# Gate and convolution projections as 2x2 blocks with seven products, kept in DRAM, ahead of the merges

## Chip, cores and metric

One core of a Trainium2 chip runs the whole kernel. The metric is the device time of one execution in microseconds (us). TensorE (PE) multiplies; VectorE (DVE), ScalarE (ACT) and GpSimd (POOL) work element by element; the queue of SyncE (SP) issues the transfers. 0.2% is 4.2 us.

## The reference

One layer on a sequence of 1024 rows of 1024 floats. Everything is float32.

```
h = rms_norm(x, norm1_g)
a_b, a_c, a_x, q, kv, nsa_g, pool_in, sgu_in, merge_g = split_columns(h @ w_in)
out_a = a_b * causal_dwconv(a_c * a_x, conv_a_w)          # 512 wide
out_b = nsa_mixer(q, kv, nsa_g, ...)                      # attention, 512 wide
out_c = pool_mixer(pool_in, pool_w, pool_scale)
out_d = spatial_gating(sgu_in, sgu_norm_g, sgu_w, sgu_b)
gm = sigmoid(merge_g.reshape(b, s, 4, d))                 # four gates, 1024 wide each
merged = sum(gm[:, :, i] * (out_i @ w_branch[i]) for i in range(4))
x = x + merged @ w_o
gate, up = split(rms_norm(x, norm2_g) @ w_up)
x = x + (silu(causal_dwconv(gate, conv_ff_w)) * up) @ w_down
```

## The kernel before

A float32 product is made of three matmuls: each operand is split into a high part (ACT copies it to fp32r, suffix `_h`) and a low part (DVE subtracts, suffix `_l`), and high by high, high by low and low by high are summed in PSUM. PSUM has 8 banks of 128x512; two banks hold one output tile of 128 columns of weights by the 1024 rows of the sequence.

The order is: norm and projections for attention, attention, then a middle part, then the feed-forward part `ff`. The middle part is a table `STAGES` of (name, weight pieces, chunks): merge1, conv, merge0, v, pool, merge2, u, merge3, wo. A **chunk** is one output tile. With 8 k-tiles (a product of `h` with 128 columns of `w_in`: a gate, or an input of conv, pool or u) it has 2 x 8 x 3 = 48 matmuls of 128x512; with 4 k-tiles (a branch's output with 128 columns of `w_branch`) it has 24. A merge has 8 output tiles. For each it multiplies a gate chunk and then a branch chunk; ACT takes the sigmoid out of PSUM into `sig_all` (L1036; `sig_0` in merge0), DVE multiplies it with the branch chunk in two halves (L1590) and adds it to `merged` (L1596).

Weights come through two slots of `raw`, and from there into two slots of `ring_h` (ACT, `high_ring`, L1019) and `ring_l` (DVE, `low_ring`, L1571). Pieces alternate between the slots. The semaphores count: `pl_done` the low parts (SP loads piece m when piece m-2 has its low part, and PE waits for the one that it needs), `mm_done` the chunks, `freed` the chunks whose banks have been read, `acc_done` the tiles added to `merged`. Four pairs of banks rotate over the chunks. Stage v needs four whole pieces in `wv_h` and `wv_l` before its first matmul; in the last turn of merge0 ACT and DVE prepare them (`value_weights`) beside the last gate chunk. In the last turn of merge3, DVE prepares the first pieces of `w_o` in the same way.

Attention is a list of slots written out by hand; the last seven have only the values, the turns and the sums of earlier scores (L2125 to L2127, L2169, L2178). PE then waits for `ol_done`, and the first piece of merge1 gets its high and low part.

The feed-forward part already has the scheme that the change uses elsewhere: a 2x2 block product of two column tiles with seven products in place of eight (`seven`, L2405). Sums and differences of the blocks of `h` are made once (`t1` to `t4`), those of each pair of weight tiles by POOL (L798, L826), and results of the products are carried over between banks by ACT and DVE (`seed_done`, `fe_done`, `upper_done`, `other_done`). There PE multiplies `down` tiles between the seven products.

Of the kernel before, what the change touches and what calls it, by code (L numbers as in the profile page):

```python
# [72 lines left out]
DIRECT = 2  # L73
SEVENS = FT - DIRECT
# [3 lines left out]
class Chain:  # L78
# [20 lines left out]
    def link(self, ins):  # L99
# [5 lines left out]
STAGES = (("merge1", 16, 16), ("conv", 12, 12), ("merge0", 16, 16), ("v", 4, 0), ("pool", 4, 4), ("merge2", 16, 16),  # L105
          ("u", 4, 4), ("merge3", 16, 16), ("wo", 8, 0), ("ff", 0, 0))
# [9 lines left out]


# [80 lines left out]
def build(nc, x, norm1_g, w_in, conv_a_w, qk_norm_g, cmp_pe, cmp_w1, cmp_w2, pool_w, pool_scale,  # L198
# [13 lines left out]
    with ExitStack() as ctx:  # L212
# [44 lines left out]

        ring_h = place("ring_h", 104, [P, 2, 1024], F32R)
# [4 lines left out]
        conv_c = place("conv_c", 160, [P, 2, S], F32)  # L263
        conv_u = place("conv_u", 168, [P, 2, S + 2], F32)
        conv_o = place("conv_o", 176.25, [P, 2, S], F32)

        sig_0 = place("sig_0", 184.25, [P, 2, S], F32)
# [93 lines left out]

        x_loaded = [sem(f"x_loaded{t}") for t in range(TT)]
# [18 lines left out]
        ones_made = sem("ones_made")  # L381
# [15 lines left out]
        pe_loaded = sem("pe_loaded")  # L397
# [30 lines left out]
        convc_done = sem("convc_done")  # L428
# [37 lines left out]
        seed_done = sem("seed_done")  # L466
        fe_done = sem("fe_done")
        upper_done = sem("upper_done")
        other_done = sem("other_done")
# [9 lines left out]
        tdiff_done = sem("tdiff_done")  # L479
        xw_done = sem("xw_done")  # L480
        th_done = sem("th_done")
        tl_done = sem("tl_done")
# [4 lines left out]
        passed = sem("passed")  # L487
# [69 lines left out]

        def corner(a, k0, half):

            return a[:, k0:k0 + 4, half * HALF:(half + 1) * HALF]  # L560
# [15 lines left out]
        def _(sp):  # L576
# [26 lines left out]
            for b in range(P // L16):  # L603
                sp.dma_start(pe_rows[b * L16:(b + 1) * L16, :, :, :],
                             cmp_pe[0].rearrange("j (h l) d -> l j h d", h=2)).then_inc(pe_loaded, 16)
# [18 lines left out]
            def load(m, slot, dst, src):  # L624

                sp.wait_ge(pl_done, m + 1)
                sp.sem_inc(passed, 1)
                sp.dma_start(dst, src).then_inc(piece_loaded[slot], 16)
# [15 lines left out]
            sp.wait_ge(s_done, unit_of_tile(1, 5) + 1)  # L644
            with sp.Fori(0, KT // 2) as t:
                load_merge(1, t, PIECE["merge1"])
            for c in range(3 * BK):
                col = (BW, 2 * BW, 0)[c % 3] + (c // 3) * P
                load(PIECE["conv"] + c, c % 2, ring_piece(c % 2), w_in_k[:, :, col:col + P])
            with sp.Fori(0, KT // 2) as t:  # L650
                load_merge(0, t, PIECE["merge0"])
# [9 lines left out]
            with sp.Fori(0, KT // 2) as t:  # L661
                load_merge(2, t, PIECE["merge2"])
# [7 lines left out]
            with sp.Fori(0, KT // 2) as t:  # L670
                load_merge(3, t, PIECE["merge3"])
# [3 lines left out]
            sp.wait_ge(mgl_done, 1)  # L675
# [41 lines left out]
        def _(pool):  # L717
# [22 lines left out]
            def place_added(T):  # L740
                pool.wait_ge(qn_done, T + 1)
                after(pool, qkT_done, 0, T - 1)
                if T == 0:
                    pool.wait_ge(pe_loaded, 16 * (P // L16))
# [59 lines left out]
            pool.wait_ge(xw_done, 4)  # L804
            for k in range(4):
                minus(t3_f[:, k, :], t3_f[:, k, :], t1_p[:, k, :]).then_inc(tdiff_done, 1)
            for k in range(4):
                plus(t1_f[:, k, :], b11[0][:, k, :].bitcast(F32), b11[1][:, k, :].bitcast(F32)).then_inc(tdiff_done, 1)
            for k in range(4):
                pool.wait_ge(tdiff_done, 4 + k + 1)  # L810
                plus(t2_f[:, k, :], t3_f[:, k, :], t1_f[:, k, :]).then_inc(tdiff_done, 1)
            for k in range(4):
                minus(t1_f[:, k, :], t1_p[:, k, :], t1_f[:, k, :]).then_inc(tdiff_done, 1)
            for k in range(4):
                plus(t4_f[:, k, :], b21[0][:, k, :].bitcast(F32), b21[1][:, k, :].bitcast(F32)).then_inc(tdiff_done, 1)
            for k in range(4):
                pool.wait_ge(tdiff_done, 16 + k + 1)
                minus(t4_f[:, k, :], t4_f[:, k, :], t2_f[:, k, :]).then_inc(tdiff_done, 1)
# [16 lines left out]
        def _(act):  # L835
# [102 lines left out]
            for T in range(LAST):  # L938
# [21 lines left out]
                if T + 3 < TT:  # L960
                    input_root(T + 3)
            projected(LAST)
# [4 lines left out]
            for slot in slots:  # L967
# [14 lines left out]
                if slot["n"] == KEYS_1 + 1:  # L982
                    compressed_keys(1, 6)
                if slot["unit"]:
# [22 lines left out]
            act.wait_ge(pv_done, UNITS)  # L1007
# [6 lines left out]
            def high_ring(turn, per, m, c, slot, k=KT):  # L1014

                act.wait_ge(piece_loaded[slot], turn * (per // 2 * 16) + (m // 2 * 16 + 16))

                act.wait_ge(mm_done, turn * per + (c + 1))
                nc.scalar.activation(ring_h[:, slot, 0:k * P], raw[:, slot, 0:k * P], ACT.Copy).then_inc(ph_done, 1)  # L1019

            def merge(b, turn, m0, c0, t0, last=False, beside=None, beside_at=0):

                sig = sig_0 if b == 0 else sig_all
                for a in range(2):
                    for p in (2 * a, 2 * a + 1):
                        if not (last and p == 3):

                            nxt = m0 + p + 1 + (4 if b == 0 and beside and p == 3 else 0)
                            high_ring(turn, 4, nxt, c0 + p + 1, (p + 1) % 2, KT if p % 2 else BK)
                        if p == 2 * a:  # L1030
                            if beside and a == beside_at:
                                beside()

                            act.wait_ge(mm_done, turn * 4 + (2 + c0 + p + 1))
                            act.wait_ge(acc_done, turn * 2 + (t0 + a + 1))
                            nc.scalar.activation(sig[:, a, :], flat[:, p * 1024:(p + 1) * 1024],  # L1036
                                    ACT.Sigmoid).then_inc(sig_done, 1)

            high_ring(0, 4, 0, 0, 0)
            with act.Fori(0, KT // 2) as t:  # L1040
                merge(1, t, PIECE["merge1"], CHUNK["merge1"], 0)

            for c in range(3 * BK):
                m, ck_ = PIECE["conv"] + c, CHUNK["conv"] + c
                high_ring(0, 4, m + 1, ck_ + 1, (c + 1) % 2)
                q = c // 3
# [1417 lines left out]
```

## Time and profile before

| | |
|---|---|
| median of 3 runs | 2107.41 us (2105.77 to 2107.66) |
| the profiled execution | 2107.77 us |
| its span, first to last instruction | 2106.1 us |
| TensorE granted clock, mean | 0.991 |

A matmul of 128x512 is shown as 390 ns long; matmuls overlap, so what one costs is the distance between the starts of two. "Idle before" names what ended an engine's wait.

### The profile page before, as it was taken

The numbers are of one execution on the slowest core, as the hardware profiler recorded it, in microseconds if no ns is written. First come the engines' busy times: TensorE is split into PE (matmuls) and PEld (weight loads), VectorE is DVE, ScalarE is ACT, GpSimd is POOL, SyncE is SP. The second block draws the span as 40 slices with busy tenths as digits, with TensorE's granted clock in tenths as the row PEclk, the third lists the DMA queues.
The fourth block names the chain that finished last, engine by engine and source line by source line (L and its number), as shares of the span: only waits on it lengthen the run. The fifth ranks groups of instructions, "written<-read, shape, count | busy, mean of one in ns | idle before, by whom it ended". The sixth has DMA issues, their size and how long they took to land.

```text
span 2106.1 us, 26839 instructions
## 1 busy us (share of the span) xinstructions
PE 2049.4 (97%) x9737; PEld 1658.3 (79%) x9737; DVE 1178.0 (56%) x1869; ACT 734.8 (35%) x1191; POOL 258.2 (12%) x222
## 2 busy tenths in 40 slices
PE   7999999998999999999999999999999999999998
PEld 7897566665888888888788888877788888888886
DVE  6857677765222232235424322447877777777777
ACT  4534666665221111122212321324323333333332
POOL 2001224321000000000000000006211111111110
PEclk9999999999999999999999999999999999999999
DMA  6200000000112111111112121501112211221212
GB/s 168 52 2 1 1 1 1 1 16 16 45 45 61 50 39 46 45 50 50 46 45 71 29 55 46 179 17 44 41 50 60 60 40 51 59 60 40 57 52 90
DMA packets 149241, 98.98 MB, mean 47 GB/s; under 512 B 22747, under 2 KB 140717, under 8 KB 149165
## 3 DMA queue, kind: packets, MB, share of 16 engines
q1 hardware_dynamic: 147597, 97.57, 16.3%
q8 instruction: 47, 0.77, 0.2%
q10 hardware_dynamic: 1568, 0.39, 0.1%
q14 instruction: 29, 0.24, 0.0%
HBM read 93.76 MB, written 4.19 MB: 47 GB/s over the span
## 4 chain that ended last, share of the span: by engine, by line
PE 75%; DVE 2%; POOL 2%; ACT 1%; issue 0%; DVEq 0%; PEldq 0%; ACTq 0%; POOLq 0%
PE bank L2207 12%; PE bank L2209 12%; PE bank L2208 12%; PE bank L2360 11%; PE bank L2368 6%; PE bank L2369 6%; PE bank L2370 6%; PE bank L2309 4%; POOL t_f L802 1%; PE bank L2258 1%; PE bank L2259 1%; PE bank L2257 1%; DVE x L1839 1%; POOL t_f L798 1%; PE bank L2125 0%; PE bank L2105 0%
## 5 line engine op out<-in xcount | busy, mean ns | idle before, releaser
L2207 PE MATMUL bank<-actT_h,ring_h 128*128 128x512 f32 x832 | 325.3, 391 | 3.5 <-DVE ring_l L1571 3.5
L2208 PE MATMUL bank<-actT_l,ring_h 128*128 128x512 f32 x832 | 324.7, 390 | 0.0
L2209 PE MATMUL bank<-actT_h,ring_l 128*128 128x512 f32 x832 | 324.6, 390 | 0.0
L1571 DVE TENSOR_TENSOR ring_l<-raw,ring_h 128x1024 fp32r<-128x1024 f32 x84 | 85.6, 1019 | 354.2 <-ACT ring_h L1019 354.0
L1839 DVE TENSOR_TENSOR x<-x,bank 128x1024 f32<-128x1024 f32 x176 | 212.4, 1216 | 38.9 <-PE bank L2360 38.9
L2207 PEld LDWEIGHTS bank<-actT_h,ring_h 128*128 128x128 f32 x832 | 156.7, 188 | 36.1 <-issue 3.7
L2209 PEld LDWEIGHTS bank<-actT_h,ring_l 128*128 128x128 f32 x832 | 156.7, 188 | 32.6
L2208 PEld LDWEIGHTS bank<-actT_l,ring_h 128*128 128x128 f32 x832 | 156.7, 188 | 32.4
L990 ACT ACTIVATE pT<-bank 128x512 f32<-128x512 f32 (+1 forms) x148 | 88.3, 596 | 108.0 <-PE bank L2110 105.4
L2368 PE MATMUL bank<-t_h,block_h 128*128 128x512 f32 x320 | 124.8, 390 | 0.8 <-ACT ffd L1211 0.8
L2370 PE MATMUL bank<-t_h,block_l 128*128 128x512 f32 x320 | 124.7, 390 | 0.0
L2369 PE MATMUL bank<-t_l,block_h 128*128 128x512 f32 x320 | 124.6, 390 | 0.0
L2368 PE MATMUL bank<-actT_h,block_h 128*128 128x512 f32 x304 | 120.1, 395 | 3.4 <-DVE actT_l L1812 3.0
L2369 PE MATMUL bank<-actT_l,block_h 128*128 128x512 f32 x304 | 119.5, 393 | 0.0
L2370 PE MATMUL bank<-actT_h,block_l 128*128 128x512 f32 x304 | 119.4, 393 | 0.0
L1019 ACT ACTIVATE ring_h<-raw 128x1024 fp32r<-128x1024 f32 x84 | 74.9, 891 | 127.6 <-PE bank L2209 124.8
L1425 DVE TENSOR_REDUCE nmx<-bank 128x1 f32<-128x512 f32 (+4 forms) x154 | 96.0, 637 | 39.1 <-PE bank L2036 29.3
L1514 DVE TENSOR_TENSOR pT_l<-pT,pT_h 128x512 fp32r<-128x512 f32 (+1 forms) x148 | 106.4, 719 | 15.5 <-ACT pT_h L993 15.3
L2360 PE MATMUL bank<-wd_h,ffa_h 128*128 128x512 f32 x352 | 109.4, 392 | 5.7 <-DVE x L1839 3.5
L2360 PE MATMUL bank<-wd_l,ffa_h 128*128 128x512 f32 x352 | 108.6, 390 | 0.0
L2360 PE MATMUL bank<-wd_h,ffa_l 128*128 128x512 f32 x352 | 108.5, 390 | 0.0
L993 ACT ACTIVATE pT_h<-pT 128x512 fp32r<-128x512 f32 (+1 forms) x148 | 93.5, 631 | 4.7
(350 smaller groups left out, 4164.2 us busy)
## 6 DMA issues: line engine op xcount, KB each, us to landing
raw<-in_w_in SPq DMA_DIRECT2D x60, 512.0 KB, 3.8
raw<-in_w_up SPq DMA_DIRECT2D x44, 512.0 KB, 5.0
wd_raw<-in_w_down SPq DMA_DIRECT2D x22, 512.0 KB, 3.6
raw<-in_w_branch SPq DMA_DIRECT2D x32, 256.0 KB, 2.8
x_in<-in_x SPq DMA_DIRECT2D x8, 512.0 KB, 4.5
raw<-in_w_o SPq DMA_DIRECT2D x8, 512.0 KB, 3.6
x<-in_x SPq DMA_DIRECT2D x8, 512.0 KB, 8.9
out<-x SPq DMA_DIRECT2D x8, 512.0 KB, 2.6
```

The costliest lines, as they stand in the source:

```text
L990: nc.scalar.activation(pT[0:nr, u % RING, :], bank[0:nr, 3 + u % 2, :], ACT.Exp).then_inc(exp_done, 1)
L993: nc.scalar.activation(pT_h[0:nr, u % RING, :], pT[0:nr, u % RING, :], ACT.Copy).then_inc(pth_done, 1)
L1425: nc.vector.tensor_reduce(nmx[:, n % MAXIMA, c // HALF, r0:r0 + heads], bank[:, 7 if at < EARLY else at % 2, 0:heads * w].rearrange("p (r ...
L1514: nc.vector.tensor_tensor(pT_l[0:nr, u % RING, :], pT[0:nr, u % RING, :], pT_h[0:nr, u % RING, :].bitcast(F32), ALU.subtract).then_inc(ptl ...
L1839: nc.vector.tensor_tensor(x2[:, t, :], x2[:, t, :], flat[:, (2 + t % 2) * 1024:(3 + t % 2) * 1024], ALU.add).then_inc(d_done, 1)
L2207: nc.tensor.matmul(o, wh(k), ah(k)[:, cols], start=k == 0, stop=False)
L2208: nc.tensor.matmul(o, wh(k), al(k)[:, cols], start=False, stop=False)
L2209: ins = nc.tensor.matmul(o, wl(k), ah(k)[:, cols], start=False, stop=k == k_tiles - 1)
L2360: ins = nc.tensor.matmul(o[h], av, w[:, h * HALF:(h + 1) * HALF], start=n == 0, stop=n == 2)
L2368: nc.tensor.matmul(o, wh, b[0][:, k, :], start=start and k == 0, stop=False, skip_group_check=seeded)
L2369: nc.tensor.matmul(o, wh, b[1][:, k, :], start=False, stop=False, skip_group_check=seeded)
L2370: ins = nc.tensor.matmul(o, wl, b[0][:, k, :], start=False, stop=stop and k == 3, skip_group_check=seeded)
```

## The change

All four gates (but the first two tiles of merge2's and merge3's) and the twelve tiles of the conv are multiplied in one stage behind attention. Its unit is a pair of column tiles: 20 pairs, 14 of gates, 4 of `taps` (a tile of a_c with its tile of a_x) and 2 of `outs` (two tiles of a_b). A pair is a 2x2 block product: eight products of 12 matmuls in the first two pairs (`PLAIN`), seven in the other 18. Pairs alternate between two sets of four banks and between `raw` and a second buffer `raw2`. Seven of the plain products stand one by one in the last seven attention slots. The sigmoids and the conv's outputs are stored to DRAM (`gates_kept`, `conv_kept`) and loaded again, one 512 KB tile at a time, when a merge needs them; `gate_load` waits until the tile before the last one has been added to `merged`.

Merge1 and merge0 then have 8 branch chunks each and nothing else; merge2 and merge3 have two gate chunks, as before, and 8 branch chunks. A weight piece of a branch now holds two column tiles (512 KB). The loops are written out. `value_weights` stands behind the last tile of merge0, on ACT and on DVE. Semaphores of the feed-forward part are renamed and start from an offset; the eight small loads of `pe_rows` count on the semaphore of the constants. Below is the core of the diff: table, SP, ACT, DVE, PE in this order.

```diff
-STAGES = (("merge1", 16, 16), ("conv", 12, 12), ("merge0", 16, 16), ("v", 4, 0), ("pool", 4, 4), ("merge2", 16, 16),
-          ("u", 4, 4), ("merge3", 16, 16), ("wo", 8, 0), ("ff", 0, 0))
+STAGES = (("merge1", 4, 8), ("merge0", 4, 8), ("v", 4, 0), ("pool", 4, 4), ("merge2", 6, 10), ("u", 4, 4),
+          ("merge3", 6, 10), ("wo", 8, 0), ("ff", 0, 0))
...
+PAIRS = ([("gate", b, m) for b in (1, 0) for m in (0, 2, 4, 6)]
+         + [("taps", 0, 0), ("taps", 0, 1), ("outs", 0, 0), ("taps", 0, 2), ("taps", 0, 3), ("outs", 0, 2)]
+         + [("gate", b, m) for b in (2, 3) for m in (2, 4, 6)])
+NPAIR = len(PAIRS)
+PLAIN = 2
...
+        gates_kept = nc.dram_tensor("gates_kept", (4, KT, P, S), F32, kind="Internal").ap()
+        conv_kept = nc.dram_tensor("conv_kept", (BK, P, S), F32, kind="Internal").ap()
...
+            def gate_load(b, i, sig):
+                m = i % KT
+                sp.wait_ge(acc_done, i + 1)
+                sp.dma_start(sig[:, m % 2, :], gates_kept[b, m]).then_inc(sig_loaded[m % 2], 16)
...
+            sp.wait_ge(pair_low, pair_operand(NPAIR - 2) + 6)
+            sp.wait_ge(pair_side, 4 * (NPAIR - 2 - PLAIN) + 4)
+            branch_load(1, PIECE["merge1"], 0)
+            pair_store(NPAIR - 1)
+            branch_load(1, PIECE["merge1"] + 1, 1)
+            sp.wait_ge(pair_mm, len(PRODUCTS))
+            for i in range(4):
+                sp.wait_ge(kept_stored[i], 16 * stores_until(NPAIR, i))
...
+            def later_merge(b):
+                m0 = PIECE[f"merge{b}"]
+                for a in range(2):
+                    col = COL_MERGE + b * DM + a * P
+                    load(m0 + 2 * a, 0, ring_piece(0), w_in_k[:, :, col:col + P])
+                    branch_load(b, m0 + 1 + 2 * a, a)
+                if b == 2:
+                    sp.wait_ge(poold_done, BK)
+                else:
+                    sp.wait_ge(mix_mm, TT)
+                for p in range(2, 4):
+                    gate_load(b, b * KT + 2 * p - 2, sig_all)
+                    gate_load(b, b * KT + 2 * p - 1, sig_all)
+                    branch_load(b, m0 + 2 + p, p)
+
+            later_merge(2)
+            gate_load(2, 2 * KT + 6, sig_all)
+            gate_load(2, 2 * KT + 7, sig_all)
...
+            c0, m0 = CHUNK["merge1"], PIECE["merge1"]
+            act.wait_ge(pair_mm, pair_product(NPAIR - 1) + 3)
+            high_ring(m0, c0)
+            high_ring(m0 + 1, c0)
...
+            def later_merge(b, last, beside=None):
+                m0, c0 = PIECE[f"merge{b}"], CHUNK[f"merge{b}"]
+                high_ring(m0 + 1, c0 + 1)
+                if beside:
+                    beside()
+                in_place(b, 0, 0)
+                high_ring(m0 + 2, c0 + 2)
+                high_ring(m0 + 3, c0 + 5)
+                in_place(b, 1, 1)
+                high_ring(m0 + 4, c0 + 5)
+                high_ring(m0 + 5, c0 + 7)
+                if not last:
+                    high_ring(m0 + 6, c0 + 9)
...
+            c0, m0 = CHUNK["merge0"], PIECE["merge0"]
+            for m in range(KT):
+                gated_branch(0, m, c0 + m)
+                if m in (1, 3):
+                    low_ring(m0 + 2 + m // 2)
             def value_weights():
                 for c in range(4):
-                    low(0, 4, PIECE["v"] + c, wv_l[:, 2 * c:2 * c + 2, :],
+                    low(PIECE["v"] + c, wv_l[:, 2 * c:2 * c + 2, :],
                             raw[:, c % 2, :].rearrange("p (k n) -> p k n", k=2),
                         wv_h[:, 2 * c:2 * c + 2, :])
 
-            with dve.Fori(0, KT // 2 - 1) as t:
-                merge(0, t, PIECE["merge0"], CHUNK["merge0"], KT)
-            merge(0, KT // 2 - 1, PIECE["merge0"], CHUNK["merge0"], KT, beside=value_weights, beside_at=1)
-
+            value_weights()
...
+            def later_merge(b, beside=None, beside_chunk=None):
+                m0, c0 = PIECE[f"merge{b}"], CHUNK[f"merge{b}"]
+                low_ring(m0 + 1)
+                if beside:
+                    beside()
+                low_ring(m0 + 2)
+                gated_branch(b, 0, c0 + 1, own_gate=True)
+                low_ring(m0 + 3)
+                gated_branch(b, 1, c0 + 3, own_gate=True)
+                low_ring(m0 + 4)
+                for m in range(2, KT):
+                    gated_branch(b, m, c0 + 2 + m)
+                    if m == 3:
+                        low_ring(m0 + 5)
+                    if m == 5 and b == 2:
+                        low_ring(m0 + 6)
+                    if beside_chunk:
+                        beside_chunk(m)
...
+            def with_chunk(m):
+                if 4 <= m < KT:
+                    merged_low(m - 4)
+                if m in (5, 6):
+                    output_low(m - 5)
...
+            def pair_step(k):
+
+                u, j = PRODUCTS[k]
+                n = pair_operand(u) + j
+                if j == 0:
+                    after(pe, pair_act, 0, evacuations(u - 1, 0))
+                    after(pe, pair_dve, 0, evacuations(u - 1, 1))
+                if j == 1:
+                    after(pe, pair_fe, 0, u - PLAIN - 1)
+                if j == 2:
+                    pe.wait_ge(pair_seed, u - PLAIN + 1)
+                if j == 4:
+                    pe.wait_ge(pair_upper, u - PLAIN + 1)
+                if j == 6:
+                    pe.wait_ge(pair_other, u - PLAIN + 1)
+                if u == PLAIN and j in (1, 2, 4, 5):
+                    pe.wait_ge(dl_done, {1: 4, 2: 8, 4: 12, 5: 16}[j])
+                pe.wait_ge(pair_low, n + 1)
+                role = (0, 3, 1, 0, 1, 2, 1)[j]
+                pair_block_product(pair_bank(u, role), n, (b11, d3, d2, b21, d1, d4, b22)[j], j < 2, j != 0 or True,
+                                   seeded=j >= 2)
...
+            def branch_chunk(m, c, j, oh, ol, tile):
+                pe.wait_ge(pl_done, 2 + m + 1)
+                pe.wait_ge(freed, c + 1)
+                slot = m % 2
+                product(BK, lambda k: ring_h[:, slot, (2 * k + j) * P:(2 * k + j + 1) * P],
+                        lambda k: ring_l[:, slot, (2 * k + j) * P:(2 * k + j + 1) * P],
+                        oh, ol, 2 * tile).then_inc(mm_done, 1)
...
+            def later_merge(b, beside=None):
+                m0, c0 = PIECE[f"merge{b}"], CHUNK[f"merge{b}"]
                 for a in range(2):
-                    chunk(turn, m0 + 2 * a, c0 + 2 * a, 0, KT, act_h, act_l, 2 * a)
-                    if beside and a == 0:
-                        beside()
-                    if branch_ready:
-                        pe.wait_ge(obl_done, branch_ready)
-                    chunk(turn, m0 + 2 * a + 1, c0 + 2 * a + 1, 1, BK, oh, ol, 2 * a + 1)
+                    chunk(m0 + 2 * a, c0 + 2 * a, 2 * a)
+                    if a == 0:
+                        if beside:
+                            beside()
+                        pe.wait_ge(obl_done, b * BK)
+                    branch_chunk(m0 + 1, c0 + 2 * a + 1, a, out_h, out_l, 2 * a + 1)
+                for m in range(2, KT):
+                    branch_chunk(m0 + 2 + m // 2, c0 + 2 + m, m % 2, out_h, out_l, (2 + m) % 4)
...
```

## Rows read from the trace of the kernel before

**Rows 1.** The page, busy time and share of the span of each engine.

```profile
PE 2049.4 (97%) x9737; PEld 1658.3 (79%) x9737; DVE 1178.0 (56%) x1869; ACT 734.8 (35%) x1191; POOL 258.2 (12%) x222
```

**Rows 2.** Windows, the middle part: length, each engine's busy time, granted clock, DMA share, GB/s.

```profile
520.30:1293.00 772.70, 769.58 (x3428) 638.43 (x3429) 247.85 (x293) 163.82 (x178) 0.78 (x2) 1.00 0.18 49
```

**Rows 3.** The page, costliest groups: one form of the middle part's chunks.

```profile
L2207 PE MATMUL bank<-actT_h,ring_h 128*128 128x512 f32 x832 | 325.3, 391 | 3.5 <-DVE ring_l L1571 3.5
```

**Rows 4.** Timeline of ACT in stage v, one read for each 24 matmuls: start, length.

```profile
924.80 0.60 ACT L1069 ACTIVATE sgu_v<-bank 128x512 f32<-128x512 f32 x1 [3.50 <-PE bank L2259]
...
935.68 0.60 ACT L1069 ACTIVATE sgu_v<-bank 128x512 f32<-128x512 f32 x1 [4.84 <-PE bank L2259]
```

**Rows 5.** Timeline where attention ends and merge1 starts; in brackets the wait and its cause.

```profile
513.46 0.44 PE L2169 MATMUL bank<-ident,oT 65*128 65x65 f32 x4 [1.02 <-DVE o_gated L1557]
...
516.42 0.44 PE L2178 MATMUL bank<-ident,o_gated 128*128 128x128 f32 x2 [2.53 <-POOL o_gated L784]
...
518.99 1.23 DVE L1571 TENSOR_TENSOR ring_l<-raw,ring_h 128x1024 fp32r<-128x1024 f32 x1 [1.25 <-ACT ring_h L1019]
...
520.35 0.79 PE L2207 MATMUL bank<-actT_h,ring_h 128*128 128x512 f32 x1 [3.49 <-DVE ring_l L1571]
...
523.84 0.39 PE L2209 MATMUL bank<-actT_h,ring_l 128*128 128x512 f32 x1
```

**Rows 6.** Groups by line: high part, low part and POOL's sum of 128x512 in ff.

```profile
L1152 ACT ACTIVATE block_h<-side 128x512 fp32r<-128x512 f32 x80 | 50.2, 628 | 100.5 <-PE bank L2370 100.5
...
L1761 DVE TENSOR_TENSOR block_l<-side,block_h 128x512 fp32r<-128x512 f32 x80 | 55.1, 689 | 13.2 <-ACT block_h L1152 13.1
...
L798 POOL TENSOR_TENSOR side<-raw 128x512 f32<-128x512 f32 x20 | 26.8, 1342 | 226.2 <-DMA raw<-in_w_up 226.2
```

**Rows 7.** Timeline of PE and ACT where a gate chunk of merge3 ends.

```profile
1322.04 0.39 PE L2207 MATMUL bank<-outb_h,ring_h 128*128 128x512 f32 x1
...
1322.24 1.03 ACT L1036 ACTIVATE sig_all<-bank 128x1024 f32<-128x1024 f32 x1 [10.19 <-PE bank L2209]
...
1323.16 1.05 ACT L1132 ACTIVATE actT_h<-merged 128x1024 fp32r<-128x1024 f32 x1
```

**Rows 8.** Timeline of DVE at the end of merge0 and the weights of v.

```profile
897.67 1.29 DVE L1590 TENSOR_TENSOR sig<-sig,bank 128x512 f32<-128x512 f32 x2 [2.28 <-PE bank L2209]
899.00 1.23 DVE L1596 TENSOR_TENSOR merged<-merged,sig 128x1024 f32<-128x1024 f32 x1
...
900.74 1.22 DVE L1571 TENSOR_TENSOR wv_l<-raw,wv_h 128x1024 fp32r<-128x1024 f32 x1
...
905.66 1.22 DVE L1571 TENSOR_TENSOR wv_l<-raw,wv_h 128x1024 fp32r<-128x1024 f32 x1 [3.70 <-ACT wv_h L1012]
...
911.63 1.23 DVE L1571 TENSOR_TENSOR wv_l<-raw,wv_h 128x1024 fp32r<-128x1024 f32 x1 [2.59 <-ACT wv_h L1012]
```

**Rows 9.** Timeline of ACT there, the third and fourth piece.

```profile
906.72 1.06 ACT L1012 ACTIVATE wv_h<-raw 128x1024 fp32r<-128x1024 f32 x1 [1.10 <-DMA raw<-in_w_in]
...
910.54 1.06 ACT L1012 ACTIVATE wv_h<-raw 128x1024 fp32r<-128x1024 f32 x1 [2.75 <-DMA raw<-in_w_in]
```

**Rows 10.** DMA issues: count, size, median us from issue to landing.

```profile
raw<-in_w_branch SPq DMA_DIRECT2D x32, 256.0 KB, 2.8
...
raw<-in_w_o SPq DMA_DIRECT2D x8, 512.0 KB, 3.6
...
sgu_w<-in_sgu_w SPq DMA_DIRECT2D x1, 256.0 KB, 5.6
```

**Rows 11.** Timeline of SP's queue at the end of merge2.

```profile
1113.83 0.35 SPq L664 DMA_DIRECT2D sgu_g<-in_sgu_norm_g  x1
...
1114.70 0.43 SPq L667 DMA_DIRECT2D sgu_w<-in_sgu_w  x1
```

**Rows 12.** Windows, a wait of PE and a stretch shortly after it.

```profile
1018.00:1020.60 2.60, 0.13 (x1) 0.00 (x0) 1.28 (x1) 2.40 (x3) 0.00 (x0) 1.00 0.35 101
...
1022.20:1025.60 3.40, 3.40 (x10) 2.71 (x9) 1.22 (x1) 0.36 (x1) 0.00 (x0) 0.52 0.12 14
```

More of the change, by code:

```diff
@@ L73 @@
 DIRECT = 2
+SEVENTHS = 18
+DIFFS = 16
 SEVENS = FT - DIRECT
@@ L478, in build @@
         wdl_done = sem("wdl_done")
[L479 to L482, printed above, removed]
         d_mm = sem("d_mm")
@@ new lines, in _ @@
+            for i in range(4):
+                sp.wait_ge(kept_stored[i], 16 * stores_until(NPAIR, i))
+            gate_load(1, 0, sig_all)
+            gate_load(1, 1, sig_all)
+            conv_load(0)
+            conv_load(1)
+            for p in range(4):
+                if p < 2:
+                    branch_load(1, PIECE["merge1"] + p + 2, p + 2)
+                else:
+                    branch_load(0, PIECE["merge0"] + p - 2, p - 2)
+                if p < 3:
+                    gate_load(1, 2 * p + 2, sig_all)
+                    gate_load(1, 2 * p + 3, sig_all)
+                if p < 2:
+                    conv_load(p + 2)
@@ L652, in _ @@
+            for p in range(4):
+                gate_load(0, KT + 2 * p, sig_0)
+                gate_load(0, KT + 2 * p + 1, sig_0)
+                if p < 2:
+                    branch_load(0, PIECE["merge0"] + p + 2, p + 2)
             for c in range(4):
@@ L1012, in high @@
                 nc.scalar.activation(dst, src, ACT.Copy).then_inc(ph_done, 1)
[L1014 to L1031, printed above, removed]
-                                beside()
[L1034 to L1037, printed above, removed]
@@ L1123, in _ @@
             gate_out(BK - 1)
[L1124 to L1129 removed]
+            later_merge(3, True)
+            act.wait_ge(mm_done, 2 + CHUNK["merge3"] + 3)
             for k in range(KT):
@@ new lines, in _ @@
+            c0, m0 = CHUNK["merge1"], PIECE["merge1"]
+            low_ring(m0)
+            low_ring(m0 + 1)
+            low_conv(0)
+            low_conv(1)
+            for i in range(2):
+                dve.wait_ge(kept_stored[i], 16 * stores_until(NPAIR, i))
+            for m in range(KT):
+                gated_branch(1, m, c0 + m)
+                if m % 2:
+                    low_ring(m0 + 2 + m // 2)
+                if m in (1, 3):
+                    low_conv(2 + m // 2)
+            c0, m0 = CHUNK["merge0"], PIECE["merge0"]
@@ L1642, in _ @@
-            merge(0, KT // 2 - 1, PIECE["merge0"], CHUNK["merge0"], KT, beside=value_weights, beside_at=1)
+            value_weights()
+            low_ring(PIECE["pool"])
             for t in range(TT):
@@ L1736, in _ @@
             gate_low(BK - 1)
-            with dve.Fori(0, KT // 2 - 1) as t:
-                merge(3, t, PIECE["merge3"], CHUNK["merge3"], 3 * KT)
             def merged_low(k):
@@ L2228, in _, with chunk @@
-            pe.sem_inc(mm_done, 2)
-            with pe.Fori(0, KT // 2) as t:
-                merge(t, PIECE["merge1"], CHUNK["merge1"], 0, oh=heads_h, ol=heads_l)
-            for c in range(3 * BK):
-                chunk(0, PIECE["conv"] + c, CHUNK["conv"] + c, c % 2, KT, act_h, act_l, (CHUNK["conv"] + c) % 4)
-            with pe.Fori(0, KT // 2) as t:
-                merge(t, PIECE["merge0"], CHUNK["merge0"], BK)
+            def chunk(m, c, tile):
+                pe.wait_ge(pl_done, 2 + m + 1)
+                pe.wait_ge(freed, c + 1)
+                slot = m % 2
+                product(KT, lambda k: ring_h[:, slot, k * P:(k + 1) * P], lambda k: ring_l[:, slot, k * P:(k + 1) * P],
+                        act_h, act_l, 2 * tile).then_inc(mm_done, 1)
@@ L2301, in _ @@
             pe.wait_ge(freed, 4 + CHUNK["merge3"] - 1)
-            with pe.Fori(0, KT // 2) as t:
-                merge(t, PIECE["merge3"], CHUNK["merge3"], 3 * BK)
+            later_merge(3, beside=lambda: (pe.wait_ge(mb_done, TT), pe.wait_ge(freed, 4 + CHUNK["merge3"])))
             def output_products(t, k, first_bank):
```

687 lines of the change are left out of this document (508 added, 179 removed).

## The prediction

> **What bounds the kernel now.** I read the page first: PE is busy for 97% of the span, every other engine for 56% or less [rows 1]. The windows then show the part that the change touches: in 772.7 us from the first merge matmul on, PE is busy for 769.6, at the full clock [rows 2]. So neither ACT, DVE nor the transfers cost anything there, and time falls only with matmuls removed, or with the few waits at the edges. It rises where a wait of PE is added. The groups give 390 ns for a matmul [rows 3], but that is length and not cost: ACT reads two outputs of stage v 10.88 us apart, with 48 matmuls between them [rows 4], so one costs 0.2267 us. A gate chunk costs 10.88, a branch chunk 5.44, and a product of 12 matmuls 2.72.
>
> **What is removed.** 18 pairs have 84 matmuls in place of 96: 216 less, 216 x 0.2267 = 49.0 us. Where pairs of gates or tiles are merely moved, the count stays.
>
> **The end of attention.** PE waits 1.02, 2.53 and 3.49 us there, 7.0 in all, and then eight starts take 3.49 us at the low clock where 1.81 are due [rows 5]. Seven plain products, 19 us of work that depends on none of this, now stand between these slots, so all 8.7 us are covered. Against it, ACT and DVE get four operands to split in the last full slots, at 0.63 and 0.69 each [rows 6]; they are not the bound there, so I charge 0.5. Bounds 0 and 4 x 0.63 = 2.5. Gain 8.2, between 6.2 and 8.7.
>
> **The pair stage itself.** Per seven-product pair PE has 19.0 us. ACT has seven high parts, two bank copies of about 0.6 and sigmoids of about 2.2, some 8 us; DVE seven low parts and two additions, some 6.5, in a conv pair some 12; POOL four sums of 1.3 [rows 6]. The carried results decide: each has one product, 2.72 us, of cover (the seed is read one product later, so are the upper and the other sum). For the seed, ACT has after the last product of a pair one high part and a sigmoid of 1.03, done 2 us later, then copies 0.6: it is in time by 1.9 us. I cost the stage at nothing beside its matmuls. If that cover is short by d, it costs 18 x d.
>
> **Pair stage to merge1.** ACT takes the last sigmoid before it touches the first branch piece. From the end of the last product: 0.2 to ACT's start and 1.03 of sigmoid [rows 7], which is awaited; high part 1.05 [rows 7], low part 1.23, reaction of PE 0.1 [rows 5]. Wait 3.7 us.
>
> **Merge1 and merge0.** A branch chunk of 5.44 needs one 512 KB gate and half a 512 KB piece. DVE needs 1.3 for the multiplications and 1.2 for the addition [rows 8]. A gate is asked for when the tile two before it is done, 10.9 us ahead less 2.7; a lone 512 KB takes 3.6 [rows 10], two together up to 4.8 (below). This fits, with some 3 us to spare, and four pairs of banks take up what DVE loses on the conv's pieces. Cost 0.
>
> **Stage v.** All four lows of `value_weights` now follow the last tile of merge0 on DVE. Counted from the end of its last matmul: start 0.2 [rows 7], multiplications 1.33, addition 1.23, two low parts of 1.22 [rows 8], of which the first ends at 4.0 and the second at 5.1 (back to back they overlap a little). Only then may pieces 3 and 4 be loaded. In the trace a low part's end and the next high part's start in that slot are 906.88 and 910.54, 3.66 us, and 901.96 and 906.72, 4.76 us, where two loads overlap [rows 8, 9]. So piece 4 lands at 5.1 + 4.8 = 9.9, high part 1.06, low part 1.23, PE at 12.3. Before, this lay beside a gate chunk. Wait 12.3, at least 11.1 with 3.66.
>
> **Merge2 and merge3.** The second branch piece (tiles 2 and 3) goes to slot 1, which the fourth chunk still reads. PE wants it at once: 0.2 + 1.05 + 1.23 + 0.1 = 2.6 us of wait. From there, with time 0 at the end of the fourth chunk, the order on SP and DVE sets the pace. DVE has tile 1 added at 5.0. SP then issues the gate of tile 3 and behind it the piece of tiles 4 and 5, which lands at 10.2; DVE stands in its low part until 12.5 and adds tiles 2 and 3 until 17.6. The next piece is again behind a gate and lands at 22.8, low part at 25.1; PE wanted it at 24.4. Wait 0.8. Tile 5 is added at 30.0.
> In merge2, SP now issues the last gate, three constants and only then the first piece of u, and DVE stands before tile 6 until that piece is split. The constants took from 1113.83 to 1114.70 + 5.6 = 1120.3, 6.5 us [rows 10, 11]; the piece lands at about 30.4 + 6.5 + 1.7 = 38.6, split 40.9, tile 6 multiplied at 42.1. PE was done at 36.1. Wait 6.2. Merge2 costs 9.6.
> In merge3, DVE must have the second part of `merged` and the first of `w_o` before tile 6. The piece of `w_o` lands at 36.3, four operations on it end at 40.7, PE was done at 36.1: wait 4.7. PE then does half of the first step, 2.7, and needs tile 7's banks, multiplied at 46.6: wait 3.3. Merge3 costs 11.4. Later pieces of `w_o` keep ahead of steps of 5.44.
>
> **The clock.** A wait of 2.5 us was followed by a stretch of 3.4 us at 0.52 of the full clock [rows 12], the level of 1.2 GHz: 3.4 x 0.48 = 1.6 us lost. I charge 1.6 at four places (merge1, v, u, wo), 6.4; the dips after the waits of 2.6 fall into a stretch that DVE paces anyway. Bounds 3 and 13.
>
> **Sum.** -49.0 - 8.2 + 3.7 + 12.3 + 9.6 + 11.4 + 6.4 = -13.8. The profiled execution took 2107.8 (span 2106.1 and 1.7 around it), 0.4 above the median: 2107.4 - 13.8 = 2093.6.
>
> The landings are the softest row. [...]
>
> Elsewhere: the constants' semaphore waits for eight small loads more, which are long in before it is read; the renamed semaphores of `ff` move no wait. Both cost nothing.
>
> **Rivals.** (1) *Carried results arrive late in the pair stage.* PE would wait in each of 18 pairs; from 0.8 us per pair on the gain is gone, and at 2 us the time is 2094 + 36 = 2130. For it: no `down` tile stands between products any more. Against: ACT and DVE are half idle and I find 1.9 us of slack. 7%. (2) *The merges are paced by gates from DRAM.* Gates, pieces and conv outputs share one queue; if a gate takes 9 us in place of 5, each of 14 branch chunks in merge1 and merge0 gains 1 to 2 us, and 2094 becomes about 2112. For it: 4.76 when two overlap; against: the stretch has 786 KB per 5.44 us to move, 145 GB/s, and loads that came strictly one behind another at 3.6 us [rows 10] would carry 146; they overlap. 8%. (3) *The waits don't arise*, since pieces come early or DVE is ahead: only -57 remains, 2050; half of them gone is 2072. For it: no such wait in the trace now. Against: the order on DVE and SP is fixed by the code and the durations by rows. 8%. (4) *The clock falls oftener*, at all nine waits and for longer: 2100. 10%.
>
> **Numbers.** The forecast as worked out, 2084 to 2104, has 67%. What a measurement can tell from no change is 0.2%, 4.2 us: faster is below 2103.2. Faster: forecast 65, rival 3 8, rival 4 9, mild forms of rivals 1 and 2 2: 84%. Same: 8% (forecast 2, rival 4 1, rivals 1 and 2 5). Slower: 8%, the rest of rivals 1 and 2. The range reaches down to half of rival 3 and up to the edge of rival 2: 2079 to 2106.
>
> **What would show it.** Right: 1704 matmuls of pairs with no wait above 1 us; one wait of some 12 us before the first matmul of v, released by the low part of the fourth piece; 6 before the first chunk of u and 5 and 3 at the first step of `w_o`, released by DVE; DVE's idle time ended by ACT's high parts and these by loads. Wrong: PE waiting inside pairs for ACT's bank copies, DVE waiting for gates in merge1 and merge0, or the clock below 1 over long stretches.

## The result and the profile after

The changed kernel takes 2114.52 us (median of 8 runs, 2111.04 to 2115.59), the kernel before 2107.74 us (8 runs, 2105.53 to 2109.49): a ratio of 1.0031, 95% interval 1.0020 to 1.0042. It is slower by about 6.5 us (4 to 9) where 13.8 us less was forecast. The profiled execution took 2111.34 us, with a span of 2109.6. One execution of the first experiment below took 5640 us; its ratio leaves it out, and the cause isn't known.

The page of the changed kernel, busy time of the engines, beside [rows 1]:

```profile
span 2109.6 us, 26451 instructions
PE 2016.2 (96%) x9521; PEld 1625.9 (77%) x9521; DVE 1288.9 (61%) x2012; ACT 786.5 (37%) x1323; POOL 386.6 (18%) x310
```

PE has the 216 matmuls less, yet the span is 3.5 us longer. So PE stands or runs slowly elsewhere. PE's waits in this kernel, by the instruction that ended them:

```profile
PE bank L2384 <- DVE xn L1649: 12.8, 8, 9.9
PE bank L2758 <- DVE wv_l L1980: 12.1, 1, 12.1
PE bank L2682 <- DVE ring_l L1980: 8.8, 3, 3.9
PE bank L2550 <- DVE pair_l L1831: 7.8, 2, 7.3
PE bank L2682 <- DVE sig_all L2003: 7.7, 1, 7.7
...
PE bank L2806 <- issue: 3.7, 1, 3.7
PE bank L2550 <- DVE bank L1943: 3.5, 1, 3.5
...
PE bank L2806 <- DVE sig_all L2003: 1.5, 1, 1.5
```

The first row belongs to the projections and stands in both kernels. Each of the others shown is new, 45.1 us in all: at v (L2758), at merge1 and in merge2 and merge3 (L2682 for `ring_l`), before u (`sig_all`), at w_o (L2806) and, not forecast, 11.3 us at L2550 in the pair stage. Behind eight of the nine waits of over 2 us between 550 and 1340 us the granted clock falls; the ninth, 2.5 us for `outb_l`, has no slow stretch behind it here. Windows from PE's restart to the end of each slow stretch (length, busy time and instructions of PE, PEld, DVE, ACT and POOL, granted clock, share of DMA time, GB/s), beside [rows 12]:

```profile
563.80:569.70 5.90, 5.90 (x14) 4.55 (x15) 5.90 (x4) 2.89 (x5) 5.90 (x4) 0.50 0.44 178
583.50:586.90 3.40, 3.40 (x10) 2.61 (x9) 0.41 (x1) 0.33 (x1) 0.91 (x1) 0.51 0.60 151
919.90:924.80 4.90, 4.90 (x12) 3.84 (x13) 1.23 (x1) 1.06 (x1) 0.00 (x0) 0.50 0.94 330
1021.60:1027.20 5.60, 5.60 (x13) 4.38 (x14) 1.23 (x1) 1.06 (x1) 0.00 (x0) 0.50 0.11 34
1157.20:1160.50 3.30, 3.30 (x10) 2.57 (x9) 0.98 (x1) 0.00 (x0) 0.00 (x0) 0.52 0.38 107
1197.80:1201.10 3.30, 3.08 (x7) 2.48 (x8) 3.23 (x5) 0.49 (x1) 0.00 (x0) 0.50 0.61 159
1290.10:1293.30 3.20, 3.20 (x9) 2.42 (x9) 2.11 (x3) 0.00 (x0) 0.00 (x0) 0.50 0.06 8
1328.20:1331.10 2.90, 2.90 (x7) 2.32 (x8) 2.87 (x4) 0.00 (x0) 0.00 (x0) 0.51 0.54 181
```

The lengths add up to 32.5 us at the level of 1.2 GHz, half of them lost: 16.2 us. The kernel before lost 1.6 in this stretch [rows 12], besides 1.7 at attention's end [rows 5].

The account between two points that both kernels have, the last score matmul of attention (508.61 us before, 508.46 after) and the first matmul of `ff` (1422.3 and 1426.1), where the changed kernel takes 4.0 us more:

| term | forecast | measured |
|---|---|---|
| 216 matmuls less | -49.0 | -49.0 |
| end of attention | -8.2 | -8.7 |
| waits in the pair stage | 0 | +11.3 |
| merge1 | +3.7 | +3.9 |
| v | +12.3 | +12.1 |
| merge2 with u | +9.6 | +10.2 |
| merge3 with w_o | +11.4 | +7.7 |
| clock | +6.4 | +14.6 |
| sum | -13.8 | +2.1 |

1.9 us remain unassigned. The rows of waits and clock aren't independent: a slow stretch can fill time in which PE would have waited (see merge2 and merge3 below). From `ff` on both are equal within 0.3 us. The changed kernel's median is 3.2 us above its profiled execution, and no trace shows where. Other executions of this family differ ahead of the changed part as well: in two of the experiments below PE waits 2.0 us for `kcAB` early in attention, and in the others it doesn't.

**Where the unforeseen 11.3 us are.** VectorE and GpSimd in the changed kernel while the blocks of differences of the input are made (timeline: start, length, engine, line; "xcount" after several instructions in a row):

```profile
533.38 2.49 DVE L1888 TENSOR_TENSOR d_p<-actT_h,actT_l 128x512 f32<-128x512 f32 x4
536.35 0.69 DVE L1831 TENSOR_TENSOR pair_l<-raw,pair_h 128x512 fp32r<-128x512 f32 x1 [0.48 <-ACT pair_h L1188]
536.96 18.28 DVE L1888 TENSOR_TENSOR d_f<-actT_h,actT_l 128x512 f32<-128x512 f32 x12
555.16 6.78 DVE L1894 TENSOR_TENSOR d_l<-d_f,d_h 128x512 fp32r<-128x512 f32 x4
561.87 1.74 DVE L1831 TENSOR_TENSOR pair_l<-raw,pair_h 128x512 fp32r<-128x512 f32 x1
```

```profile
537.72 6.77 POOL L966 TENSOR_TENSOR d_f<-d_f,d_p 128x512 f32<-128x512 f32 x4 [14.43 <-DVE d_f L1888]
544.45 6.84 POOL L966 TENSOR_TENSOR d_f<-d_f 128x512 f32<-128x512 f32 x4
```

```profile
548.43 0.63 ACT L1188 ACTIVATE pair_h<-raw 128x512 fp32r<-128x512 f32 x1 [3.27 <-PE bank L2552]
```

```profile
563.75 0.76 PE L2550 MATMUL bank<-actT_h,pair_h 128*128 128x512 f32 x1 [7.26 <-DVE pair_l L1831]
```

Four additions take 2.49 us while GpSimd is idle. The next twelve, the same operation on the same shape, take 18.28, and GpSimd's four differences 6.77 where a sum of this size takes 1.34 alone [rows 6]. The high part of the weights is ready at 549.06. Its low part stands in VectorE's queue behind the additions and four low parts of the differences until 561.87, and PE waits.

The Trainium skill has this ("SBUF — State Buffer", section "Who interferes with whom"): a VectorE instruction with both inputs in SBUF and a GpSimd instruction that reads SBUF exclude each other for a whole instruction, they don't share. The trace agrees: from 538 us on one VectorE instruction runs to each of GpSimd's, both with a pitch (start to start) of about 1.7 us. That is some 0.2 us less than 0.61 and 1.29 us, what the two take alone, add up to.

### The profile page after: what moved, and what is told of

Its sections match the earlier page's. It is cut to its first block, busy times and chain, and to the rows that moved or that the text cites. A ratio compares the mean times of both kernels' runs of the same rounds, so it can differ in the third digit from the quotient of the medians.

```text
span 2109.6 us, 26451 instructions
## 1 busy us (share of the span) xinstructions
PE 2016.2 (96%) x9521; PEld 1625.9 (77%) x9521; DVE 1288.9 (61%) x2012; ACT 786.5 (37%) x1323; POOL 386.6 (18%) x310
## 4 chain that ended last, share of the span: by engine, by line
PE 69%; DVE 5%; DMA 2%; issue 1%; ACT 1%; SPq 0%; POOL 0%; DVEq 0%; ACTq 0%; POOLq 0%
PE bank L2857 11%; PE bank L2865 6%; PE bank L2866 6%; PE bank L2867 6%; PE bank L2550 6%; PE bank L2551 6%; PE bank L2552 6%; PE bank L2682 4%; PE bank L2683 4%; PE bank L2684 4%; PE bank L2806 4%; PE bank L2758 1%; PE bank L2760 1%; PE bank L2759 1%; DMA raw<-in_w_branch 1%
## 5 line engine op out<-in xcount | busy, mean ns | idle before, releaser
L2550 PE MATMUL bank<-actT_h,pair_h 128*128 128x512 f32 x280 | 110.4, 394 | 7.8 <-DVE pair_l L1831 7.8
L2550 PE MATMUL bank<-d_h,pair_h 128*128 128x512 f32 x288 | 113.1, 393 | 3.5 <-DVE bank L1943 3.5
L1831 DVE TENSOR_TENSOR pair_l<-raw,pair_h 128x512 fp32r<-128x512 f32 x62 | 54.4, 877 | 96.2 <-ACT pair_h L1188 96.1
L2551 PE MATMUL bank<-d_l,pair_h 128*128 128x512 f32 x288 | 112.9, 392 | 0.0
L2552 PE MATMUL bank<-d_h,pair_l 128*128 128x512 f32 x288 | 112.6, 391 | 0.0
L2551 PE MATMUL bank<-actT_l,pair_h 128*128 128x512 f32 x280 | 109.9, 393 | 0.0
L2552 PE MATMUL bank<-actT_h,pair_l 128*128 128x512 f32 x280 | 109.9, 393 | 0.0
L944 POOL TENSOR_TENSOR shift<-ident,nmx 128x512 fp32r<-128x512 f32 x48 | 66.6, 1388 | 196.0 <-DVE nmx L1737 111.5
L1980 DVE TENSOR_TENSOR ring_l<-raw,ring_h 128x1024 fp32r<-128x1024 f32 x28 | 34.3, 1223 | 111.5 <-ACT ring_h L1331 110.8
```

What stands on the lines that cost most here:

```text
L2550: nc.tensor.matmul(out, wh, b[0][:, kt, :], start=start and kt == 0, stop=False, skip_group_check=seeded)
L2551: nc.tensor.matmul(out, wh, b[1][:, kt, :], start=False, stop=False, skip_group_check=seeded)
L2552: ins = nc.tensor.matmul(out, wl, b[0][:, kt, :], start=False, stop=stop and kt == 3, skip_group_check=seeded)
```

## Experiments

Ratios are to the kernel before, run on the same chip, with their 95% intervals; 0.001 is 2.1 us. What each gained against the changed kernel is the difference to 1.0031; with both intervals it is uncertain by some 3 us, so the causes below rest on the traces. Edits are shown condensed: loops are written out and lines left out.

### The end of the pair stage

```diff
+ # ScalarE, last pair, ahead of the last sigmoid; the same three lines behind the loop are gone
+ act.wait_ge(piece_loaded[m % 2], m // 2 * 16 + 16)
+ act.wait_ge(pair_mm, pair_product(NPAIR - 1) + 3)
+ nc.scalar.activation(ring_h[:, m % 2, :], raw[:, m % 2, :], ACT.Copy).then_inc(ph_done, 1)
  pair_gate(u, 0)
```

> Edit: ScalarE splits the first branch piece before the last gate's sigmoid instead of behind it. Theory (each wait of TensorE and the slow stretch behind it cost what the trace shows, and go with their cause): the wait of 3.9 us at the first merge matmul is gone, and with it the 2.5 us that the clock costs after it: 6.4 us less than the changed kernel, so about 0.4 us over the kernel before. Rival (the wait only moves): the third chunk then waits for the banks of the last sigmoid, now 1.05 us later, and the clock falls there: less than 2 us gained. Rival (clock): the wait goes but the clock falls in this stretch all the same: 3.9 us gained, not 6.4.

Measured: 2109.35 us, ratio 1.0016 (1.0006 to 1.0026), 3.2 us gained. PE there:

```profile
918.74 0.47 PE L2688 MATMUL bank<-outg_h,ring_h 128*128 128x512 f32 x1 [0.98 <-DVE ring_l L1986]
```

The wait fell from 3.9 to 1.0: two sigmoids of the last pair still stood ahead. The 2.5 us of slow clock are gone too. Against these 5.4 us, a slow stretch of 3.4 us (1.7 lost) now follows the later wait of 2.5 us for `outb_l`, which the changed kernel has without one. The stretch behind merge2's wait of 2.5 us (1.6 lost) is missing in turn, and there PE waits 0.60 us for a branch piece and 8.1 us before u, where the changed kernel has no wait and 7.7. In the pair stage this execution waits 12.0 us instead of 11.3. The first theory holds for the wait. That less than the forecast 6.4 us arrived fits these small changes, none of which an experiment isolates.

### The value weights beside merge0

```diff
  # SyncE, per pair of tiles of merge0
  gate_load(0, KT + 2 * p, sig_0)
+ if p >= 2: value_load(2 * p - 4)
  gate_load(0, KT + 2 * p + 1, sig_0)
+ if p >= 2: value_load(2 * p - 3)
  # VectorE, per tile
  gated_branch(0, m, c0 + m)
+ if 3 <= m < 7: value_low(m - 3)
```

> Edit: the four pieces of the sgu's value weights are loaded among the gates of merge0 and split beside its tiles 3 to 6, not behind its last tile. Theory (waits and slow stretches are additive): the 12.1 us wait before the first matmul of v is gone, and with it 2.8 us at the low clock: 14.9 us less than the changed kernel, about 8 us under the kernel before. Rival (the queue and VectorE are full there): loads among the gates delay these and VectorE's 3.9 us per tile of 5.44 comes late, so that tiles 4 to 7 each make TensorE wait 1 to 3 us: 5 us or less gained.

Measured: 2099.89 us, ratio 0.9972 (0.9962 to 0.9981), 12.4 us gained. All that PE waits for between the start of merge1 and the middle of v:

```profile
PE bank L2686 <- DVE ring_l L1985: 3.9, 1, 3.9
```

The wait of 12.1 is gone and no tile waits in its place. The queue and VectorE had room. Here too the wait for `outb_l` has a slow stretch behind it (1116.00 to 1119.50 at 0.56), 1.5 us. That leaves 13.4 of the 14.9 expected; the last 1.0 us to the measured 12.4 is within the uncertainty.

### The order in merge2 and merge3

```diff
  # SyncE
  gate_load(b, b * KT + 2 * p - 2, sig_all)
+ branch_load(b, m0 + 2 + p, p)
  gate_load(b, b * KT + 2 * p - 1, sig_all)
- branch_load(b, m0 + 2 + p, p)
...
+ output_piece(0)
  gate_load(3, 3 * KT + 6, sig_all)
+ output_piece(1)
  gate_load(3, 3 * KT + 7, sig_all)
  # TensorE
- chunk(m0 + 2, c0 + 2, 2)
- branch_chunk(m0 + 1, c0 + 3, 1, out_h, out_l, 3)
+ branch_chunk(m0 + 1, c0 + 2, 1, out_h, out_l, 2)
+ chunk(m0 + 2, c0 + 3, 3)
```

> Edit: in merge2 and merge3 each branch piece is asked for ahead of a gate, the second half of the first branch piece is multiplied before the second gate chunk, and the first pieces of u and w_o are loaded before the last gates. Theory (additive): the waits of 4.9 us (two), 7.7, 3.7 and 1.5 us are gone, 17.8 in all, and with them 6.4 us of low clock in four stretches: 24 us less than the changed kernel, about 17 under the kernel before. Rival (VectorE paces these stages, not the loads): the waits shrink by half and come up at the tiles instead: 8 to 12 us gained.

Measured: 2086.65 us, ratio 0.9914 (0.9898 to 0.9931), 24.6 us gained. The waits of PE from merge1 to the end of merge3:

```profile
PE bank L2768 <- DVE wv_l L1989: 12.1, 1, 12.1
PE bank L2692 <- DVE ring_l L1989: 3.9, 1, 3.9
...
PE bank L2692 <- DVE outb_l L2074: 2.5, 1, 2.5
PE bank L2757 <- issue: 0.5, 1, 0.5
```

None of the five waits (17.8 us) is left in merge2 and merge3, and no slow stretch either. VectorE doesn't pace these stages; the order does. The edit changes that of the loads and that of TensorE's chunks together, so it doesn't tell how much belongs to either. The rival falls.

### The differences on VectorE

```diff
- # GpSimd
- nc.gpsimd.tensor_tensor(out_[:, k, :], a[:, k, :], b[:, k, :], op).then_inc(diff_done, 1)
+ # VectorE, in between its additions and low parts, four per product
+ dve.wait_ge(whole_done, wholes + k + 1)
+ nc.vector.tensor_tensor(out_[:, k, :], a[:, k, :], b[:, k, :], op).then_inc(diff_done, 1)
```

> Edit: the 16 differences of blocks of the input, which GpSimd made, are made by VectorE, so that VectorE has 44 instructions there instead of 28 and GpSimd only the weights' sums. Theory (the two engines shut each other out): with GpSimd mostly idle VectorE's instructions take 0.61 to 0.69 us back to back instead of 1.6, 44 of them 27 to 30 us in a stretch of 33, and TensorE's waits of 7.3, 0.6 and 3.5 us before and in the first seven-product pair are gone, with 4.7 us at the low clock: 16 us less than the changed kernel, about 9 under the kernel before. Rival (VectorE has simply too many instructions before their due time): 16 more make the waits longer, by up to 16 x 0.69 = 11 us: 18 us over the kernel before.

Measured: 2103.45 us, ratio 0.9989 (0.9980 to 0.9999), 8.8 us gained. VectorE and GpSimd in it, groups of the stretch from 530 to 600 us (busy time, mean ns), and GpSimd's timeline:

```profile
L1872 DVE TENSOR_TENSOR d_f<-actT_h,actT_l 128x512 f32<-128x512 f32 x12 | 7.5, 681 | 0.0
L1879 DVE TENSOR_TENSOR d_f<-d_p,d_f 128x512 f32<-128x512 f32 x4 | 2.5, 683 | 0.0
L1879 DVE TENSOR_TENSOR d_f<-d_f 128x512 f32<-128x512 f32 x8 | 6.1, 818 | 0.0
```

```profile
557.12 3.48 POOL L984 TENSOR_TENSOR side<-raw,side 128x512 f32<-128x512 f32 x1 [28.73 <-DVE pair_l L1815]
560.56 1.74 POOL L972 TENSOR_TENSOR side<-raw 128x512 f32<-128x512 f32 x1
```

```profile
573.03 0.80 PE L2545 MATMUL bank<-d_h,pair_h 128*128 128x512 f32 x1 [4.42 <-DVE bank L1933]
```

Sixteen instructions more on VectorE, and PE waits 4.4 us instead of 11.3. Behind it the clock is low for 5.9 us, 2.9 lost instead of 4.7. Together that makes 8.7 us, the measured gain, where 16 were expected. (The expectation counted 28 and 44 instructions; with the first four additions they are 32 and 48.) The twelve additions take 7.5 us, not 18.3. The exclusion shows from the other side as well: GpSimd's sum that meets four additions back to back on VectorE takes 3.48 us. The rival (too many instructions) falls. The wait that stayed is another one. ScalarE stood in the high parts of the last difference, which VectorE had not made yet, and copied `pair_d` late, for which the upper sum waits. These differences took 3.59 us beside a sum of GpSimd's, where four take 2.49 alone.

### GpSimd keeps the differences, VectorE's order is changed

```diff
- if k == 8: for kt in range(4): whole(d3_f, *x22, kt)
- if k == 9: for kt in range(4): whole(d1_f, *x11, kt)
+ if k in (8, 9): whole(d3_f, *x22, kt)      # two per product
+ if k in (10, 11): whole(d1_f, *x11, kt)
```

The fourth set of additions and the low parts move back by one to two products in the same manner.

> Edit: GpSimd keeps the 16 differences; only VectorE's order changes: its 28 instructions on the input's blocks are spread over 14 products, two to four behind each low part of the weights, where they stood in front of later low parts in blocks of four. Theory (the two engines shut each other out, 28 instructions at about 1.65 us and 12 low parts are some 60 us of VectorE in 38 to 40 us): TensorE's waits before and in the first seven-product pair only change places, 8 to 12 us in all: ratio within 0.002 of the changed kernel's 1.003. Rival (only the order was wrong): the waits fall below 3 us: ratio 0.996 to 0.998.

Measured: 2111.21 us, ratio 1.0020 (1.0011 to 1.0030), 2.3 us gained. PE's waits at the pair products:

```profile
PE bank L2549 <- DVE d_l L1894: 5.5, 2, 5.3
...
PE bank L2549 <- issue: 3.6, 1, 3.6
```

With 0.6 for a low part of the weights, 9.7 us where there were 11.3. The group of twelve additions still has 18.3 us, mean 1595 ns. A gain of 2.3 us isn't clear of the uncertainty, and the rival's 3 us of waits are far off. The order mainly decides at which product PE waits. What must go is the meeting of the two engines.

### Matmuls in the place of a wait

```diff
+ pe.wait_ge(freed, 4 + CHUNK["pool"] - 2)
+ for i in range(48):
+     nc.tensor.matmul(bank[:, 0, :], actT_h[:, 0, 0:P], actT_h[:, 0, 0:HALF], start=True, stop=True)
  pe.wait_ge(pl_done, 2 + PIECE["v"] + 4)
```

> Edit: 48 matmuls that nothing reads (10.9 us at full clock) fill TensorE's wait of 12.1 us before v; the wait for the split weights itself stays as long as it was. Theory (the clock falls because TensorE stands idle): the first matmuls of v follow at the granted clock 1.00, and the 2.8 us lost there are gone; the waits elsewhere and the slow stretches behind them stay. Rival (the clock falls in this kernel at some rate whatever TensorE does, because it is kept busier by the products): the stretch of v's first 6 us is at 0.5 all the same, or another slow stretch appears within the next 50 us.

Measured: one execution, 2113.19 us, the kernel before on the same chip 2106.43. Windows over the filling, the first matmuls of v, and a stretch behind the wait for `outb_l`:

```profile
1010.00:1021.00 11.00, 11.00 (x50) 9.13 (x49) 4.78 (x5) 2.42 (x3) 0.00 (x0) 1.00 0.29 91
1024.80:1030.40 5.60, 5.60 (x25) 4.63 (x26) 1.22 (x1) 1.06 (x1) 0.00 (x0) 1.00 0.15 47
1133.00:1136.60 3.60, 3.60 (x11) 2.84 (x10) 1.23 (x1) 0.72 (x1) 0.00 (x0) 0.56 0.00 0
```

In 5.60 us behind the wait 25 matmuls are recorded, in the changed kernel 13. From the first matmul of merge1 (923.0) to the first of pool (1068.4) it takes 145.4 us instead of 148.0 (919.8 to 1067.8): 2.6 of the 2.8 us are gained, with weights that come no earlier. So at this wait the low clock followed from PE's standing still and not from how much it computes, as far as one execution can show. A stretch at 0.56 appears 108 us later, behind the wait for `outb_l`, and takes 1.7 back (the one behind merge2's wait of 2.5 us is missing in turn, and PE waits 1.2 us for the next branch piece there); the rival's limit of 50 us is passed, its idea of a return is not refuted by this one execution. The profiled time is above that of the changed kernel because this execution is 3.1 us behind already at the last score matmul of attention (511.6 against 508.46), where PE had waited 2.0 us for `kcAB`.

### All edits together

The edits of the first four experiments. Besides, the first branch piece is split before all three sigmoids of the last pair, VectorE makes the first four additions and the last difference one step earlier, and ScalarE's last high parts stand behind its copy of `pair_d`.

> Edit: the edits of the four experiments together, the first branch piece now split before all three sigmoids of the last pair, and the differences on VectorE with the last block's sum, difference and high part one step earlier on VectorE and one step later on ScalarE. Theory (additive): the matmuls saved, 49.0 us, and the 8.7 us at attention's end stay gained, less one wait of 2.5 us that the kernel before has too: 50 to 58 us under the kernel before, ratio 0.973 to 0.976, no wait of TensorE above 1 us between 510 and the end of the merges but for that one, mean granted clock back at 0.99. Rival (hidden again): removing one wait brings up the next in line, as in the experiment on the end of the pair stage, where 3.2 us came of 6.4: half of what is open comes back: about 35 us under the kernel before, ratio 0.983. Rival (clock): the clock settles lower for the denser kernel: mean 0.98 and 10 us less gained.

Measured: 2051.88 us (2051.25 to 2054.47), ratio 0.9743 (0.9730 to 0.9756): 54 us under the kernel before. PE's waits in it from the end of attention to the first products of `ff`:

```profile
PE bank L2881 <- DVE actT_l L2246: 3.0, 1, 3.0
PE bank L2698 <- DVE outb_l L2080: 2.5, 1, 2.5
PE bank L2873 <- DVE x L2273: 1.9, 1, 1.9
PE bank L2566 <- DVE d_l L1904: 1.7, 1, 1.7
PE bank L2566 <- DVE bank L1953: 1.4, 1, 1.4
PE bank L2763 <- issue: 0.5, 1, 0.5
```

The first three and the last stand in the kernel before too (its waits for `x` in `ff` are 3.5 us in three). Of the changed kernel's own waits, 3.1 us are left, at the first seven-product pair, with no slow stretch behind them; the mean granted clock is 0.993 (0.991 before, 0.981 in the changed kernel). The first theory gave 50 to 58 us; both rivals fall.

## Why the prediction was wrong

- **The matmuls and the end of attention** were right: -49.0, and 8.7 us where 8.2 were charged. No matmul of a pair waits at 510 to 524 us. The version with all edits is 54 us under the kernel before; the 49.0 and 8.7, less the 3.1 us of waits that it has left, are 54.6.
- **"The pair stage itself ... I cost the stage at nothing"** is the step that failed. For the steady pairs it holds: from 600 to 900 us PE is busy for 300.00 us at the full clock, and the slack of the carried results, on which the first rival rested, is there. But the sum left out what the stage must do once: 16 additions, 16 differences and 32 high and low parts of the input before the first seven-product pair, at the rate of one engine alone. [Rows 6] gave 0.69 and 1.34 us each. Behind the first four, VectorE's twelve additions took 1.60 us in the mean and its 16 low parts 1.29. That is 11.3 us of waits and 4.7 of slow clock behind them, 16.0 of the 17.8 by which the account misses.
- **The clock** is the second term, 14.6 us in place of 6.4. It took one stretch of 3.4 us from [rows 12] and charged it at four places. Eight waits had one, and those after 7.3, 3.9 and 12.1 us of waiting lasted 4.9 to 5.9 us. Lost in full were the 4.7 us in the pair stage, 2.5 behind merge1's wait and 2.8 behind v's, where 1.6 each were charged. 1.6 us came back by luck: the kernel before has a slow stretch behind its wait for `outb_l`, this execution of the changed kernel has none. The fourth rival had the mechanism, with 10%, but only 6 us of it.
- **Merge1 and v** were right within 0.2 us, each by a chain of durations on ScalarE, VectorE and the queue.
- **Merge3** has 7.7 us of waits for 11.4, yet its chain was right to 0.1 us. Its time 0 is the end of the fourth chunk, 1287.38 (the first row here less its wait):

```profile
1289.84 0.60 PE L2682 MATMUL bank<-outb_h,ring_h 128*128 128x512 f32 x1 [2.46 <-DVE ring_l L1980]
1310.25 1.06 ACT L1331 ACTIVATE ring_h<-raw 128x1024 fp32r<-128x1024 f32 x1 [11.84 <-DMA raw<-in_w_branch]
1323.54 1.06 ACT L1325 ACTIVATE wo_h<-raw 128x1024 fp32r<-128x1024 f32 x1 [11.27 <-DMA raw<-in_w_o]
1333.98 0.73 PE L2806 MATMUL bank<-wo_h,actT_h 128*128 128x512 f32 x2 [1.51 <-DVE sig_all L2003]
```

The pieces are in at 22.9 and 36.2 us (forecast 22.8 and 36.3), and PE has tile 7's banks at 46.6, as forecast. What differs is what PE did in that time: it lost 3.0 of the 3.7 us in the slow stretches behind its waits of 2.5 and 3.7 us, arrived later and waited less. The other 0.7 us are among what is unassigned. So the dips "fall into a stretch that DVE paces anyway" was right, and the 1.6 us charged at w_o shouldn't have been added.
- **Merge2** with 10.2 for 9.6 was right by luck. The first piece of u is in at 41.1 us after its fourth chunk, 2.5 later than worked out, and the slow stretch of 3.3 us took the place of some 1.6 us of waiting, the forecast wait of 0.8 for the last branch piece among it. In the two experiments in whose traces that stretch is missing (the end of the pair stage, the filling), PE waits 0.60 and 1.16 us for that piece.
- **Gates from DRAM** never made PE wait, in any of the eight kernels that have them.

With the pair stage costed rightly the forecast would have been -13.8 + 16.0, some +2: no change. The account measured +4.0.

## What to carry to other kernels

Work that a new scheme does once, to prepare its operands, needs its own sum with a due time and an engine each, even where the steady state has slack. Don't count on gaining time by sharing additions with both inputs in SBUF between VectorE and GpSimd: here both together were slower than VectorE alone with all of it. When matmuls are taken out, list every place where a buffer's or a queue's next use now has nothing in front of it, and charge each wait with the slow stretch behind it, unless another wait follows whose end another engine sets: there the stretch takes the place of waiting, as in merge3; the edits against such waits were worth more here (60.7 us) than the matmuls (49.0).

## What the runs showed of the hardware

- Two-input fp32 operations on 128x512 that run 0.61 us apart on VectorE and take 1.29 us on GpSimd alone run 1.7 us apart on both when they run at the same time. One GpSimd instruction took 3.48 us beside a run of VectorE's, which kept its pace (four additions in 2.49 us).
- The same wait of 2.5 us before the first `outb` matmul was followed by a slow stretch of 3.3 to 3.6 us in the kernel before and in four of the experiments (the end of the pair stage, the value weights, the filling and all edits), and by none in the changed kernel and in the other three. Which of the two it is, these runs don't explain. The stretch costs 1.5 to 1.7 us.
- 48 matmuls whose result nothing reads, put into a wait of 12.1 us, kept the clock at 1.00 in one execution and made the stretch from merge1 to pool 2.6 us shorter.
- In merge3 slow stretches ahead of waits whose end VectorE sets cost no time of their own: 3.0 us were lost to the clock, and PE had tile 7's banks at the 46.6 us worked out without them.
